# Hybrid decoder step on one core: w_out in column halves, router weights stationary, norm gains at the turn, first down product moved up

## What is computed

```
x = x + merged @ lp['w_out']
x = x + hier_moe(rmsnorm(x, lp['norm2_g']), lp)

g_logits = (xt @ lp['w_rg']).astype(f32) + lp['b_rg'].astype(f32)
e_logits = ((xt @ lp['w_rexp']).astype(f32) + lp['b_rexp'].astype(f32)).reshape(...)
...
for e in range(N_EXPERTS):
    h = jax.nn.silu(xt @ lp['w_e_gate'][e]) * (xt @ lp['w_e_up'][e])
    y = y + combine[:, e:e + 1] * (h @ lp['w_e_down'][e])
```

## Time and profile before

| | |
|---|---|
| median of 3 runs | 783.74 us (783.07 to 784.2) |
| span of the profiled execution | 783.6 us |
| PE busy | 741.4 us (95%) |
| DVE, ACT, POOL busy | 408.8, 259.2, 74.4 us |
| DMA | 190.68 MB, mean 243 GB/s |

### The profile page before, as it was taken

The page is one execution under the profiler, slowest core; times in us unless marked ns, Lnnn a source line. Parts: engine busy times, 40 slices in busy tenths (PEclk is TensorE's granted clock), DMA queues, the critical chain, the costliest instruction groups (busy, mean ns, idle before and its releaser), DMA issues.

```text
span 783.6 us, 12757 instructions
## 1 busy us (share of the span) xinstructions
PE 741.4 (95%) x5288; PEld 576.0 (74%) x5288; DVE 408.8 (52%) x755; ACT 259.2 (33%) x446; POOL 74.4 (9%) x104
## 2 busy tenths in 40 slices
PE   8999999999999999999999999999999997778884
PEld 7999999999999777899999988885333332323322
DVE  6999839986347785665154386554112111114226
ACT  5662351123486645532442341230111111100113
POOL 0100022001011111000000000011121221111100
PEclk9999999999999999999999999999999999999997
DMA  9578326434238433400260694389999999999994
GB/s 342 202 264 316 109 82 106 118 115 151 102 131 323 162 138 118 182 1 2 108 219 12 222 425 189 128 353 345 419 423 424 418 424 424 419 423 425 422 388 161
DMA packets 38143, 190.68 MB, mean 243 GB/s; under 512 B 5914, under 2 KB 7466, under 8 KB 21864
## 3 DMA queue, kind: packets, MB, share of 16 engines
q1 hardware_dynamic: 23696, 148.22, 47.8%
q0 software_dynamic: 11200, 34.98, 13.4%
q10 hardware_dynamic: 3184, 6.60, 2.3%
HBM read 176.17 MB, written 21.41 MB: 252 GB/s over the span
## 4 chain that ended last, share of the span: by engine, by line
PE 76%; DMA 14%; DVE 5%; ACT 3%; issue 1%; SPq 1%; DVEq 0%; ACTq 0%; POOLq 0%
PE ps L662 72%; DMA sb<-in_wexp 11%; PE ps L676 4%; DMA expert_rows<-sb 2%; DVE sb L2763 1%; DMA sb<-expert_rows 1%; DMA sb<-in_xT 1%; DVE sb L2298 1%; DVE sb L2284 1%; SPq L562 1%; ACT sb L1431 1%; ACT sb L1631 1%; DVE sb L2696 0%; ACT sb L1653 0%; ACT sb L1636 0%
## 5 line engine op out<-in xcount | busy, mean ns | idle before, releaser
L662 PE MATMUL ps<-sr 128*128 128x288 f32 (+3 forms) x2906 | 407.3, 300 | 3.5 <-DVE ps L2701 3.0
L662 PEld LDWEIGHTS ps<-sr 128*128 128x128 f32 (+1 forms) x2906 | 388.1, 188 | 18.6 <-issue 5.6
L662 PE MATMUL ps<-sb 128*64 128x512 f32 (+16 forms) x1984 | 296.9, 429 | 28.7 <-DMA sb<-in_wexp 18.1
L662 PEld LDWEIGHTS ps<-sb 128*64 128x64 f32 (+7 forms) x1984 | 148.0, 148 | 149.8 <-issue 124.7
L2632 DVE SCALAR_TENSOR_TENSOR sb<-sb,ps 128x256 f32<-128x256 f32 x16 | 6.7, 421 | 117.7 <-ACT sb L1830 117.7
L676 PEld LDWEIGHTS ps<-sb 128*128 128x128 f32 (+3 forms) x398 | 42.2, 140 | 31.0 <-issue 28.6
L676 PE MATMUL ps<-sb 128*128 128x128 f32 (+3 forms) x398 | 53.7, 273 | 2.3 <-issue 1.4
L2246 DVE TENSOR_TENSOR sr<-sb,sr 128x2048 fp32r<-128x2048 f32 (+1 forms) x17 | 39.3, 2320 | 29.1 <-ACT sr L1545 19.0
L2640 DVE COPY sb<-ps 128x1024 f32<-128x1024 f32 x15 | 18.4, 1225 | 54.5 <-PE ps L662 54.5
L1431 ACT ACTIVATE sb<-ps 128x576 f32<-128x576 f32 (+3 forms) x28 | 21.9, 783 | 67.4 <-PE ps L662 47.4
L2357 DVE SCALAR_TENSOR_TENSOR sb<-sb,ps 128x576 f32<-128x576 f32 x24 | 18.1, 753 | 46.5 <-PE ps L662 46.3
(11 more groups left out here) (291 smaller groups left out, 509.2 us busy)
## 6 DMA issues: line engine op xcount, KB each, us to landing
sb<-in_wexp SPq DMA_DIRECT2D x91, 1024.0 KB, 22.1
sb<-in_wstream SPq DMA_DIRECT2D x33, 1024.0 KB, 5.7
expert_rows<-sb ACTq DMA_DIRECT2D x1, 4608.0 KB, 24.9
sb<-in_mkT POOLq DMA_DIRECT2D x8, 512.0 KB, 7.7
sb<-in_mv POOLq DMA_DIRECT2D x8, 512.0 KB, 5.1
sb<-expert_rows SPq DMA_DIRECT2D x4, 1024.0 KB, 9.0
sb<-in_wexp SPq DMA_DIRECT2D x5, 768.0 KB, 25.4
sb<-in_x SPq DMA_DIRECT2D x4, 512.0 KB, 14.1
```

Of the source, the lines that this page charges most:

```text
L662: return signed(nc.tensor.matmul(*a, **kw))
```

## The change

Four things. **Column halves:** blocks 0 and 1 of w_out run over tiles 1 to 4 (tile 1's as before, one by one), then blocks 2 and 3 over tiles 1 to 4, two at once. The ring's places follow: w_out's first two blocks take chunks 8 to 11, issued after w04, the next three places 12 to 14, after w21, w22, w23, and the last two blocks 15 to 18, after w24. The low halves of tiles 1 to 4 are turned (`xa`), squared and multiplied with the router ahead of the high halves (`xb`). **Router:** its weights (64 columns, padded) are the stationary operand, even and odd kt in the two column halves of the array; a last product with M_SUM adds the halves and turns the result back. **Norm:** ACT scales the rows by the reciprocal root alone; norm2_g is multiplied in when the gathered rows are turned, by DVE in two halves, and `gate_up(i, 0)` waits for the first half only. M_G2's load and POOL's multiply are gone. **Pair 0:** down(0), with its turn, comes ahead of turn_rows(1); the last half of first_rows and the count product come behind gate_up(0, 0).

PSUM buffers follow a table: J mod 4 up to w04, then fixed by kind.

```diff
-    jobs += ["w00", "w20"]
-    for t in range(1, TT):
-        if t == 1:
-            jobs += ["w01", "w11", "x2T0", "w21", "lg0", "w31", "rk0"]
-            continue
-        jobs += [f"x2T{t - 1}", f"w0{t}", f"tb{t - 2}", f"lg{t - 1}", f"w2{t}", f"rk{t - 1}"]
-    jobs += ["x2T4", "xs", "lg4", "tb3", "rk4", "xs2", "tb4", "cnt"]
+    jobs += ["w00", "w20", "w01", "w11", "x2T0", "lT0", "w02", "lg0", "w03", "rk0", "xa1", "w04"]
+    jobs += ["xa2", "w21"]
+    for t in range(2, TT):
+        jobs += [f"xb{t - 1}", f"lT{t - 1}", f"tb{t - 2}", f"lg{t - 1}"] + ([f"xa{t + 1}"] if t + 1 < TT else [])
+        jobs += [f"rk{t - 1}", f"w2{t}"]
+    jobs += ["xb4", "lT4", "lg4", "tb3", "rk4", "xs", "tb4", "cnt"]
...
+            filled(sp, "w04")
+            for n in range(8, 12):
+                main_chunk(n)
+            for n, job in ((12, "w21"), (13, "w22"), (14, "w23")):
                 filled(sp, job)
                 main_chunk(n)
-            sp.wait_ge(w_used, NBLOCKS - 2)
-            for n in range(11, 15):
-                main_chunk(n)
-            sp.wait_ge(w_used, NBLOCKS)
+            filled(sp, "w24")
             for n in range(15, 19):
                 main_chunk(n)
...
+                for kt in kts[::2]:
+                    for x in range(2):
+                        last = mm(pat(pair(f"lT{t}"), 0, (1, R), p0=64 * x, pn=64), at(M_WR + (kt + x) * 64, (1, 64)),
+                                  at(M_X2T + (t % 2) * 1024 + (kt + x) * 128, (1, R)), start=(kt == 0), stop=(kt == KT - 2))
...
+            one_block(0)
+            one_block(1)
+            turn_h("x2T0", 0, range(KT))
+            two_blocks(0, 2, low_half)
+            logits(0, "x2T0", range(KT))
+            two_blocks(0, 2, high_half)
+            logit_sums(0)
+            two_blocks(0, 3)
             ranks(0)
+            turn_h("xa1", 1, low_half)
+            two_blocks(0, 4)
...
+                two_blocks(2, t, range(2))
+                turn_h(f"xb{t - 1}", t - 1, high_half)
+                two_blocks(2, t, range(2, 3))
+                logits(t - 1, f"xb{t - 1}", high_half)
+                table(t - 2)
+                logit_sums(t - 1)
+                two_blocks(2, t, range(3, 4))
+                if t + 1 < TT:
+                    turn_h(f"xa{t + 1}", t + 1, low_half)
+                two_blocks(2, t, range(4, 5))
+                logits(t, f"xa{t}", low_half)
+                two_blocks(2, t, range(5, 6))
                 ranks(t - 1)
+                two_blocks(2, t, range(6, KT))
...
                 if i == 0:
-                    for ps_ in (PS_X, PS_H, PS_Y):
-                        emptied(ps_)
+                    first_rows(4, high_half)
+                    counts()
...
+                if first:
+                    turn_hidden(i)
+                    down(i)
                 turn_rows(i + 1)
-                if not first:
+                if not first and not second:
                     down(i - 1)
...
+            def rows_turned(i):
+                dve.wait_ge(xt_ps, i + 1)
+                wait_pos(dve, gu_ps, i)
+                turned_half(PS_X, 0).then_inc(half_sb, 1)
+                turned_half(PS_X, 1).then_inc(xT_sb, 1)
```

More of the change, by code:

```diff
@@ L367, with plan_pairs @@
 J = plan_jobs()
-PS_X, PS_GU, PS_H, PS_Y = (J[job] % 4 for job in ("tb4", "rk4", "cnt", "xs2"))
+def plan_pairs():
+    pairs = {job: i % 4 for job, i in J.items() if i <= J["w04"]}
+    one, two, turned, logit = pairs["w03"], pairs["w04"], pairs["xa1"], pairs["rk0"]
+    assert sorted((one, two, turned, logit)) == list(range(4))
+    for t in range(1, TT):
+        pairs[f"w2{t}"] = pairs[f"xb{t}"] = pairs[f"lg{t}"] = pairs[f"rk{t}"] = one if t % 2 else two
+        pairs[f"lT{t}"] = logit
+    for job in ("xa2", "xa3", "xa4", "tb0", "tb1", "tb2", "xs"):
+        pairs[job] = turned
+    pairs.update(tb3=one, tb4=one, cnt=logit)
+    return pairs
+PAIR = plan_pairs()
+NTH = {job: sum(PAIR[other] == PAIR[job] for other in J if J[other] < J[job]) for job in J}
+TURNED = ["x2T0", "xa1", "xa2", "xb1", "xa3", "xb2", "xa4", "xb3", "xb4"]
+PS_X, PS_GU, PS_H, PS_Y = (PAIR[job] for job in ("tb4", "rk4", "cnt", "xs"))
 SEEDED = {1: PS_GU, 3: PS_Y, 4: PS_GU}
@@ L1275, in slot_weights, with body @@
                           at(O_ID, (1, WROWS[0]), pn=WROWS[0])).then_inc(slot_ps, 1)
-            def body(i, first, last):
+            def body(i, first, second, last):
                 if last:
@@ L1284, in body @@
                 if i == 0:
-                    for ps_ in (PS_X, PS_H, PS_Y):
-                        emptied(ps_)
+                    first_rows(4, high_half)
+                    counts()
                 if last:
                     own_rows(2)
-                elif not first:
+                elif not first and not second:
                     turn_hidden(i - 1)
@@ L1309, in pairs @@
                 for i in range(i0, i1):
-                    body(i, first=(i == i0), last=(i == i1 - 1))
+                    body(i, first=(i == i0), second=(i == i0 + 1), last=(i == i1 - 1))
                 down(i1 - 1)
@@ new lines, in first_square, with second_square @@
+            def first_square(t):
+                act.wait_ge(h_ready, first_h(t))
+                square(t, 0, D // 2, R_SA + t)
+                part = at(R_SA + t, (1, 1), pn=WROWS[t])
+                fn(part, part, ACT.Identity, scale=1.0 / D, bias=at(O_EPS, (1, 1), pn=WROWS[t])).then_inc(half_root, 1)
+            def second_square(t):
+                act.wait_ge(h_ready, all_h(t))
+                square(t, D // 2, D // 2, R_SS + t)
+                act.wait_ge(half_root, t)
+                root(t, bias=at(R_SA + t, (1, 1), pn=WROWS[t]))
@@ new lines, in _ @@
+            c_squares = [TT + 2]
+            low_half, high_half = range(4), range(4, KT)
+            shift(0)
+            shift(2)
+            copy_turned("x2T0", 0, range(KT))
+            act.wait_ge(h_ready, all_h(0))
+            square(0, 0, D, R_SS)
+            root(0, bias=at(O_EPS, (1, 1), pn=WROWS[0]))
+            copy_logits(0)
+            first_square(1)
+            first_square(2)
+            scaled_rows(0)
+            copy_turned("xa1", 1, low_half)
+            first_square(3)
@@ L2433, in add_h @@
             def add_h(b, t):
-                R, job, n = WROWS[t], f"w{b}{t}", 256 if t == 1 else 512
+                R, job, n = WROWS[t], f"w{b}{t}", 256 if t == 1 and b < 2 else 512
                 if b == 0:
```

298 lines of the change are left out of this document (161 added, 137 removed).

## The result

The changed kernel takes 788.97 us (median of 4 executions, 788.32 to 789.27), the kernel before, timed with it, 783.48 (783.07 to 784.2): ratio 1.0067, interval [1.0053, 1.0081]. It is slower, by 5.5 us between the medians (5.3 by the ratio), and lies outside the range that was given (780.7 to 788.0).

A forecast was written before the change was run, and what follows sets the result against it. The last 200 us were taken as bound by a full DMA stream of expert chunks, starting when chunk 20 can be issued. Stream terms -1.6 +1.4 +0.7 gave +0.5 on 783.7, so 784.2 us, range 780.7 to 788.0.

The forecast's parts named there:

- TensorE until w24: TensorE work up to w24's end: gains and losses sum to +2.8 us, so w24 ends at 523.0.
- (c): Before w02: TensorE stalls for w01's buffer, which DVE frees in its first add_h, +1.8 us.
- (b): Router logits with 64 stationary columns: -0.67 us for each of three tiles, -2.0 in all.
- (f): Before w24's end: about six more switches between full and 64 column products, 0 to 1.4 us, taken as 0.5.
- From w24 to gate_up(0,0): The stretch shrinks from 16.2 to 11.6 us; gate and up starts at 534.6 and ends at 538.3, 1.7 earlier.
- the new wait in pair 0 decides: Rival: a clock fall slows pair 0's down product, holes grow, 786.2 us (788 with first_rows); shares the 0.34 loss chance.
- -1.6: Stream: chunks 20 and 21, issued at 538.3, follow chunk 19 at once, where before a hole lasted to 541.7.
- +1.4: Stream: chunks 24 and 25 wait for the down product; a hole of 2.3 us, about 0.9 filled by gather and scatter.
- +0.7: Stream: a hole of about 0.7 us at chunks 26 and 27, released at 556.4.
- The stream gains: Rival: w02 stall, half-turn waits or switches do not appear, w24 up to 3 us earlier, 781.2 us; gain chance 0.27.
- Switches at full price: Rival: every tiling switch costs 0.23 us, +0.9 before w24 and +0.4 behind it, 785.5 us; one in ten.
- The slower side: Loss beyond 785.3 us, from the clock, the switches and the down wait together; chance 0.34.

The follow-up runs named there:

- adds_first: Changed kernel with DVE's add_h(0,1) and add_h(1,1) ahead of the split of w_out's last block: 786.46 us, ratio 1.0022.
- before_x2: Kernel before, with chunks 17 and 18 issued only after tile 4's row write has been issued: 784.14 us, ratio 1.0012.
- carrier: Changed kernel with a one-column matmul right behind gate_up(0,1) that carries the release of its two chunks: 788.94 us, ratio 1.0054.
- x2_first: Changed kernel with chunks 17 and 18 issued only after tile 4's row write has been issued: 789.24 us, ratio 1.0061.
- af_hid_write: Changed kernel with tile 1's additions early, pair 0's hidden rows ahead of the remaining counting chain, chunks 17 and 18 after tile 4's row write landed: 785.1 us, 1.0021.
- af_x2: Changed kernel with tile 1's additions ahead of the last w_out split, and chunks 17 and 18 after tile 4's row write is issued: 786.21 us, 1.0029.
- af_x2_hid: Changed kernel with tile 1's additions early, chunks 17 and 18 after tile 4's row write is issued, pair 0's hidden rows before remaining counting: 785.04 us, 1.0011.
- af_hid: Changed kernel with tile 1's additions ahead of the last w_out split and pair 0's hidden rows ahead of the remaining counting chain: 785.5 us, 1.0027.
- before_early: Kernel before with only pair 0's early hidden turn and down product, and its chunks' place in the stream: 784.53 us, ratio 1.0014.
- af_hid_car: Changed kernel with tile 1's additions early, pair 0's hidden rows before remaining counting, and a one-column product carrying gate_up(0,1)'s release: 784.85 us, 1.0015.
- af_hid_wr_car: Changed kernel with early additions, early hidden rows, chunks 17 and 18 after tile 4's row write landed, and a product carrying gate_up(0,1)'s release: 785.49 us, 1.0024.
- af_x2_hid_car: Changed kernel with early additions, early hidden rows, chunks 17 and 18 after tile 4's row write is issued, and carried gate_up(0,1) release: 784.63 us, 1.0014.

## Why the prediction was wrong

**The base.** "The profiled execution has a span of 783.6 us, 0.1 under the median" was compared with the wrong thing. The time is the span plus 1.73 to 1.98 in every execution since, so the profile of before is, by that, of an execution of about 785.4, 1.9 us above the median of its series. The changed kernel's profiled execution (788.32) is 0.65 below its own. Of the 5.5 us between the medians, 2.9 are between the two traces; the other 2.6 are which executions were profiled. A sum against a span of 783.6 can't tell 1 or 2 us of that. The traces name what may lie behind it, without showing it: the execution of before has the fall of the clock at 526 to 528, and that of the changed kernel is without the one behind w02's stall.

**TensorE until w24.** Near as a sum, 523.0 forecast and 523.6 measured, partly by luck: two errors go against each other. From the start of tile 0's turn (line below, and 468.03 after) to the issue of chunk 15, the kernel before takes 52.3 us, the changed kernel 55.6 and adds_first, which has no stall, 54.0 (467.22 to 521.25).

```profile
468.08 0.71 PE L676 MATMUL ps<-sb 64*128 64x64 f32 x8
```

So (c), the stall, is 1.5 for 1.8, and all the rest together +1.8 for +1.0. In that rest, (b) gave back less: for a tile of 128 rows the two halves of the logits take 0.59 and 0.49 from start to start and the sum 0.24, 1.3 us for an estimate of 1.11 and 1.8 before. (f) was about right: a split product of 512 columns takes 0.23 us start to start, and 0.33 when one with 64 stationary columns follows, in both kernels; six more such places (eleven for five) make 0.6 where the sum had 0.5. The rest of the 0.8 was not taken apart. What was missing is that the stall, in some executions, takes the clock along: up to 1.5 more.

**From w24 to gate_up(0,0).** The stretch is right: 12.0 us (523.49 to 535.46) for 11.6, whose own terms add up to 11.5. With the late w24 the product ends at 539.1 for 538.3, and chunk 20 is issued at 539.15, 0.9 us earlier than before (540.08) and not 1.7. Even that is the clock's doing: in before_x2, where it does not fall at 526, chunk 20 is issued at 538.41, 0.7 us ahead of the changed kernel. SP's issue at 538.42 is chunk 19, which waits for the written rows and says nothing of this product.

**Pair 0.** The place and the order of the waits were right, the sizes too small. Forecast and measured: start of gate_up(0,1) 540.1 and 541.14; end of the counting chain 545.0 and 546.1; end of the down product 550.7 and 553.2, of which 1.5 is the clock at 0.50; gate_up(1,0) 552.7 and 555.12. The forecast priced the clock only in the rival "the new wait in pair 0 decides", +2 us and a time of 786.2, and it is that rival that the trace shows, on top of the base error.

**The stream.** This is the step that failed. "-1.6" for the hole that would vanish: it did not, since chunk 19 waits for tile 4's rows, which I had land at 536 and which took 9.7 us beside four chunks (8.5 before) and landed at 538.4, and chunks 20 and 21 came at 539.15 and not at 538.3. So the memory is thin at 536 to 540 (205 and 61 GB/s) where before it was at 540 to 542 (160). "Chunks 22 and 23, issued 543.9": 547.46, since the end of gate_up(0,1) was 1 us later and its release is carried by the next instruction, which waits for VectorE. "Chunks 24 and 25, issued 550.8": 553.49, behind the slow down product. In place of -1.6 +1.4 +0.7, which make +0.5, the two traces show +2.9, the 1.3 MB missing at 562. Not each late issue is a loss by itself (carrier, x2_first and af_hid_write move a hole and gain nothing); what the experiments price are the two waits of TensorE, below.

**The rivals.** "The stream gains" is out; adds_first, which grants its first condition, is still 0.22% slower. "Switches at full price" has 0.1 us a switch against it, where it needed 0.23. The slower side had a chance of 0.34 where it should have had most.

**What is shown and what stays open.** The stall at w02 is worth 2.5 to 3.0 us, in two pairs that each ran in one series. VectorE's order in pair 0 is worth 1.2 between af_x2 and af_x2_hid, of one series; adds_first and af_hid, of two, differ by 1.0 in the median and not in favour of the edit in the ratio (1.0022, 1.0027), so its size is likely and not shown. With both gone about 1 to 2 us stay. They go with fewer bytes by 562 (34.7 to 35.0 MB against 35.1 to 35.3), and it is argued, not shown, that they come from w24's remaining 1.8 us and from pair 0's new order, worth about 1 us in the kernel before; these two were not separated further, and the router, the column halves and the norm's gain were not undone one by one.

## What to carry to other kernels

Where a full stream sets the end, count bytes moved by a fixed moment, for both kernels: an earlier release counts only if the memory would have been empty. Do not count a hole as waste before asking which small transfer lands in it; a gather that shares with the stream took more than twice as long here, and who waits for it may be the next bound. When a step is put on a release path, look at what its engine has queued before it, and move what nobody waits for behind it. Compare places in two traces from the last point up to which the programs are the same. And before comparing a sum with a median, find out what the profiled execution itself took.

## What the runs showed of the hardware

A write of 512 KB took 3.0 us with the memory idle, 4.9 with two chunks nearly done ahead of it, and 8.5 to 9.7 beside chunks, with little difference between two chunks ahead (8.6 to 8.9) and four (8.5 before, 9.3 to 9.7 in the changed kernels). A gather of 128 rows took 3.5 us beside a thin stream and 8.4 beside a full one.

The clock after a short idle stretch was not decided by its length alone. At w02 an idle time of 1.47 us was followed by a granted clock of 0.50 in two profiled executions of four. Pair 0's down product stands behind two idle times, the second 0.47 us in all kernels. With 1.56 for the first, it took 3.65 us in af_x2_hid and af_hid, while in before_early (1.57) and af_hid_write (1.56) the same product took:

```profile
544.65 5.35 PE L664 MATMUL ps<-sb 128*64 128x512 f32 x16 [0.47 <-ACT sb L1830]
...
545.60 5.35 PE L701 MATMUL ps<-sb 128*64 128x512 f32 x16 [0.47 <-ACT sb L1953]
```

On either side the traces agree: with 1.16 us it took 3.65 in all three (af_hid_car, af_hid_wr_car, af_x2_hid_car), with 1.94 to 2.35 it took 5.04 to 5.35 in all five (carrier, the changed kernel, adds_first, x2_first, af_x2). These are single executions, and no limit is read from them.

The Trainium skill (TensorE: Matmul & The Clock Gate, What's actually happening) says that the point at which the clock rises after a start varies from run to run; these rows show the same of its fall in mid-kernel. For a forecast this makes 1.5 us on a product a chance, not a term.
